# The first expert matrix in two transfers of 4 MB instead of four of 2 MB: a weight ring filled and freed by halves

## What is computed

```python
hdn = xb @ w_mlp1[e] + b_mlp1[e]          # w_mlp1[e]: 1024 x 2048, 8 MB
glu = jnp.minimum(hdn[:, :D_FF], SWIGLU_LIMIT)
lin = jnp.clip(hdn[:, D_FF:], -SWIGLU_LIMIT, SWIGLU_LIMIT)
act = glu * jax.nn.sigmoid(SWIGLU_ALPHA * glu) * (lin + 1.0)
return act @ w_mlp2[e] + b_mlp2[e]        # w_mlp2[e]: 1024 x 1024, 4 MB
```

## Time and profile before

| | us |
|---|---|
| median of 3 runs | 1193.2 (1192.66 to 1194.57) |
| the profiled execution | 1191.68 |
| its span, first to last instruction | 1189.9 |
| TensorE busy | 1093.7 (92%) |
| chain that ended last: DMA of the expert weights | 49% |
| chain: TensorE | 43% |
| mean granted TensorE clock | 0.993 |

### The profile page before, as it was taken

How to read it: one execution, slowest core, us unless ns; L and a number is a source line. 1 busy time by engine, 2 the same in 40 slices (tenths; PEclk the granted TensorE clock), 3 DMA queues, 4 the chain that set the end, 5 groups by cost and what they waited for, 6 DMA issues and landing times.

```text
span 1189.9 us, 14867 instructions
## 1 busy us (share of the span) xinstructions
PE 1093.7 (92%) x5421; PEld 493.3 (41%) x5422; DVE 367.6 (31%) x786; ACT 240.3 (20%) x332; POOL 3.6 (0%) x12
## 2 busy tenths in 40 slices
PE   9999998799999999999999999999888999999995
PEld 8888876543333333333333333333333333333332
DVE  6968773622211111111112212211111111111113
ACT  4846651301111111111111111111111111111112
POOL 1000000000000000000000000000000000000000
PEclk9999999899999999999999999999999999999998
DMA  9654447469999999999996999999999999999994
GB/s 339 197 173 150 164 146 261 195 281 428 428 430 426 431 427 428 430 427 430 429 426 256 431 425 431 428 427 432 426 429 431 425 431 427 427 432 425 430 429 188
DMA packets 45191, 439.44 MB, mean 369 GB/s; under 512 B 6044, under 2 KB 6232, under 8 KB 20504
## 3 DMA queue, kind: packets, MB, share of 16 engines
q1 hardware_dynamic: 43200, 436.16, 88.2%
q10 hardware_dynamic: 1976, 3.08, 0.8%
HBM read 438.17 MB, written 1.05 MB: 369 GB/s over the span
## 4 chain that ended last, share of the span: by engine, by line
DMA 51%; PE 43%; DVE 3%; ACT 2%; issue 1%; SPq 0%; DVEq 0%; ACTq 0%; PEldq 0%
DMA ring<-in_w_mlp_dram 49%; PE bank L964 19%; PE bank L648 8%; PE bank L989 6%; PE bank L642 2%; PE bank L817 2%; PE bank L882 2%; DMA sgm<-in_b_mlp_dram 1%; PE bank L922 1%; DMA ring<-in_w_in_dram 1%; PE bank L905 1%; ACT sgm L562 1%; ACT b1p L545 0%; PE bank L844 0%; PE bank L950 0%
## 5 line engine op out<-in xcount | busy, mean ns | idle before, releaser
L964 PE MATMUL bank<-ring,sga 128*64 128x512 f32 x2112 | 473.8, 595 | 62.2 <-DMA ring<-in_w_mlp_dram 62.2
L964 PEld LDWEIGHTS bank<-ring,sga 128*64 128x64 f32 x2112 | 146.9, 136 | 370.4 <-issue 238.0
L989 PE MATMUL bank<-ring,sgm 128*64 128x512 f32 x1056 | 233.9, 595 | 0.0
L1432 DVE TENSOR_SCALAR sga<-bank 128x512 f32<-128x512 f32 x33 | 22.8, 691 | 364.4 <-PE bank L964 364.4
L989 PEld LDWEIGHTS bank<-ring,sgm 128*64 128x64 f32 x1056 | 72.8, 137 | 136.1 <-issue 132.0
L569 ACT ACTIVATE sgm<-bank 128x512 f32<-128x512 f32 x33 | 19.7, 598 | 484.5 <-PE bank L964 484.5
L1452 DVE SCALAR_TENSOR_TENSOR moe_y_lo<-bank,slot_gate,moe_y_hi 128x512 fp32r<-128x512 f32 x33 | 24.8, 750 | 237.2 <-ACT moe_y_hi L576 237.2
L576 ACT ACTIVATE moe_y_hi<-bank,slot_gate 128x512 fp32r<-128x512 f32 x33 | 22.7, 687 | 259.3 <-PE bank L989 259.3
L882 PE MATMUL bank<-xn,hm 128*64 128x512 f32 x272 | 65.9, 605 | 1.3 <-DVE hm L1369 1.3
L1028 DVE TENSOR_TENSOR rlo<-ring,whi 128x2048 fp32r<-128x2048 f32 x26 | 58.9, 2285 | 5.6 <-ACT whi L416 5.3
L416 ACT ACTIVATE whi<-ring 128x2048 fp32r<-128x2048 f32 x26 | 49.0, 1917 | 7.4 <-PE bank L648 3.7
(11 more groups left out here) (260 smaller groups left out, 803.1 us busy)
## 6 DMA issues: line engine op xcount, KB each, us to landing
ring<-in_w_mlp_dram SPq DMA_DIRECT2D x192, 2048.0 KB, 23.5
ring<-in_w_in_dram SPq DMA_DIRECT2D x22, 1024.0 KB, 5.2
ring<-in_w_branch_dram SPq DMA_DIRECT2D x4, 1024.0 KB, 4.9
ring<-in_w_out_dram SPq DMA_DIRECT2D x4, 1024.0 KB, 4.9
xs<-in_x_dram SPq DMA_DIRECT2D x2, 512.0 KB, 3.8
out_dram<-xn ACTq DMA_DIRECT2D x2, 512.0 KB, 2.7
sgm<-in_b_mlp_dram ACTq DMA_DIRECT2D x3, 256.0 KB, 9.3
cst<-table_dram SPq DMA_DIRECT2D x1, 754.0 KB, 13.7
```

The lines of the kernel that those rows point to most:

```text
L964: last = mm(B[4 + u][g * C:(g + 1) * C, :], xgT[:, k % 4, k // 4, :], ring[:, q, u * FF + g * N:u * FF + (g + 1) * N], start=False, stop=( ...
L989: last = mm(B[7][g * C:(g + 1) * C, :], actT[:, j, h * C:(h + 1) * C], ring[:, q + j // 2, (j % 2) * D + g * N:(j % 2) * D + (g + 1) * N], ...
```

## The change

In `expert()` the first matrix goes in two transfers, each over two pairs (4 slots, one row of 32 KB per partition), and each waits until all four slots are freed; the second matrix goes as before. TensorE waits for landing at k = 0 and k = 4 alone, and counts four slots used at k = 3 and k = 7.

```diff
--- before.py
+++ after.py
@@ -73,6 +73,7 @@
 
 PAIRS = [SLOTS[Q_MOE + k] for k in range(0, PER_EXPERT, 2)]
 assert all(SLOTS[Q_MOE + 2 * i + 1] == at + 1 for i, at in enumerate(PAIRS))
+assert PAIRS[1] == PAIRS[0] + 2 and PAIRS[3] == PAIRS[2] + 2
 ROWS = 4
 
 
@@ -333,17 +334,16 @@
 
             def expert(e, freed):
 
-                for i, at in enumerate(PAIRS):
-                    sp.wait_ge(slots_used, freed(2 * i + 1))
-                    dst = ring[:, at:at + 2, :].rearrange("p a n -> p (a n)")
-                    if i < 4:
-                        g, half = i // 2, i % 2
-                        src = w_mlp1[0, e, g * N:(g + 1) * N, :].rearrange("(p s) n -> p (s n)", s=ROWS)
-                        src = src[:, half * 2 * SLOT:(half + 1) * 2 * SLOT]
-                    else:
-                        g = i - 4
-                        src = w_mlp2[0, e, g * N:(g + 1) * N, :].rearrange("(p s) n -> p (s n)", s=ROWS)
-                    sp.dma_start(dst, src).then_inc(landed[at], 16)
+                for g in range(2):
+                    at = PAIRS[2 * g]
+                    sp.wait_ge(slots_used, freed(4 * g + 3))
+                    src = w_mlp1[0, e, g * N:(g + 1) * N, :].rearrange("(p s) n -> p (s n)", s=ROWS)
+                    sp.dma_start(ring[:, at:at + HALF, :].rearrange("p a n -> p (a n)"), src).then_inc(landed[at], 16)
+                for g in range(2):
+                    at = PAIRS[4 + g]
+                    sp.wait_ge(slots_used, freed(KB + 2 * g + 1))
+                    src = w_mlp2[0, e, g * N:(g + 1) * N, :].rearrange("(p s) n -> p (s n)", s=ROWS)
+                    sp.dma_start(ring[:, at:at + 2, :].rearrange("p a n -> p (a n)"), src).then_inc(landed[at], 16)
 
             expert(0, lambda k: (Q_OUT, Q_OUT, Q_MOE)[k // 4])
             sp.wait_ge(tabled, 1)
@@ -957,15 +957,15 @@
                     if k == 1:
                         pe.wait_ge(yh_ready, i + 1)
                         pe.wait_ge(yl_ready, i + 1)
-                    if k % 2 == 0:
+                    if k % HALF == 0:
                         pe.wait_ge(landed[q], e * 16 + 16 * (loads_before(Q_MOE + k) + 1))
                     for u in range(2):
                         for g in range(2):
                             last = mm(B[4 + u][g * C:(g + 1) * C, :], xgT[:, k % 4, k // 4, :],
                                       ring[:, q, u * FF + g * N:u * FF + (g + 1) * N],
                                       start=False, stop=(k == KB - 1), skip_group_check=True)
-                    if k % 2:
-                        last.then_inc(slots_used, 2)
+                    if k % HALF == HALF - 1:
+                        last.then_inc(slots_used, HALF)
                 scatter(scat)
                 gather(2 * i + 4)
```

## The result

The change is slower: 1210.07 us in the median of 4 runs (1208.72 to 1210.80) against 1193.88 before (4 runs, 1192.66 to 1195.31), a ratio of 1.013 with a 95% interval of 1.0112 to 1.0147. The forecast was 1207.5, in a range of 1200 to 1213.

What follows compares the result with a forecast made beforehand. It took the saturated expert-weight DMA stream, with TensorE's work at its starts and ends, as the bound. 13.7 - 4.3 + 4.9 = +14.3 us on the profiled 1191.7 gave 1206.0, or 1207.5 against the median; range 1200 to 1213.

Steps and rivals of the forecast that it cites:

- First release: At item 0 and the second pass, the DMA idles 3.43 us longer until four slots are free: +6.9 us.
- Landing by halves: At expert 13's first pass and expert 31, 32 matmuls instead of 16 follow the last needed landing: +6.9 us.
- Longer rows: In the weight stream, 16 fewer packets per engine and expert and two fewer completions save 0.14 us per expert: -4.3 us.
- the ring: The expert-weight part from the first item on: 13.7 us lost by halves less 4.3 gained by longer rows.
- The bias load: In the front part, b_mlp1 lands later because it shares the engines with the first expert's longer rows: +4.9 us.
- each of the seven turns is 0.61 us longer: Per engine, seven weight rows alternate with bias rows; 32 KB rows lengthen the bias load's wait by 4.3 us.
- The rows already under way: Weight rows ahead of the first bias row took up to 2.7 us, and that may double.
- The bound itself: Upper limit on the bias delay: +7 us, as traffic beside it is over by 212.9 us.
- A: Rival at the front part: the bias load is not delayed, giving 1202.6 us; chance 0.20.
- B: Rival in the queue: 32 KB rows go as two packets, no gain or bias loss, 1206.6 us; chance 0.06.
- C: Rival on TensorE: its clock falls in longer waits, up to +14 us, half of it giving 1214.5; chance 0.08.
- D: Rival in the stream: a fixed cost per transfer, won back by fewer transfers, 1190.6 us at 0.35 each; chance 0.04.

Runs made afterwards that it cites:

- experiment 2: The kernel before with only SP changed, waiting until a whole half is freed, still 2 MB transfers: 1201.8 us, ratio 1.0061.
- experiment 1: The kernel before with only TensorE changed, waiting at k = 0 and k = 4 for both pairs of a half: 1202.45 us, ratio 1.0068.
- experiments 3: The kernel before with both SP and TensorE waiting for halves, still 2 MB transfers with 16 KB rows: 1208.91 us, ratio 1.0127.
- experiment 7: The change with each partition's 32 KB read as two 16 KB runs, so it does not compute the layer: 1210.31 us, ratio 1.0134.
- experiment 4: The change with the first expert's first matrix in four 2 MB transfers of 16 KB rows: 1205.45 us, ratio 1.0093.
- experiments 5 and 6: The kernel before, then the change, each issuing the first expert's weights only after the b_mlp1 copies landed: 1186.53 us and 1195.8 us.
- Experiment 8: The change with four spare matmuls on TensorE ahead of its wait at k = 4: 1208.99 us, ratio 1.0129.
- experiment 9: The kernel before with the bias landed first and first-matrix pairs 0 and 3 cut into single 1 MB slots: 1189.68 us, ratio 0.9959.

## Why the prediction was right

The four terms of the sum, one by one:

**First release, +6.9.** Right: experiment 2 gave +6.5. Together with the next term, the DMA's still time around the second pass grew from some 12 us (630.0 to 641.8) to 19 (640.4 to 659.1), by the 6.9 that were forecast.

**Landing by halves, +6.9.** Right: experiment 1 gave +7.2, both together +13.8 for the +13.7 of four times 3.43.

**Longer rows, -4.3.** Right in sign, size and cause: period 29.22 for 29.37, 4.6 us between experiments 3 and the change, and experiment 7 with the same transfers but 16 KB rows lost it again. Of the ring, 13.7 - 4.3 = 9.4 was forecast and 9.2 measured.

**The bias load, +4.9.** The mechanism was right (experiments 4 and 7), the size was short: +7.05 between the two profiles, and 7.1 by the medians of experiments 5 and 6. The mis-sized factor is "each of the seven turns is 0.61 us longer". Both queues together in the change, from 197.3 to 212.5 us:

```profile
q1 hardware_dynamic: 131, 3.77, 82.0%
q10 hardware_dynamic: 130, 0.79, 19.4%
```

131 packets of q1 are 115 rows (3.77 MB) and 16 completions, against 96 bias rows with their completions: the engines still take them one against one, and there are still some seven weight rows per engine. But a row took 82.0% x 16 x 15.2 / 115 = 1.73 us, where 16 KB took 0.93: 0.8 more, not 0.61. Bias rows were slower too: 19.4% x 16 x 15.2 / 96 = 0.49 us instead of 0.39 (27.3% x 16 x 8.6 / 96). Seven times 0.8 and six times 0.1 are 6.2 us of the 7.05.

The size differs between executions. Experiment 8 has the same transfers as the change and a piece of 17.21 us, 4.8 above that of before. From 197.3 to 210.6 us its queues have 128 packets each, 112 of them weight rows, again seven per engine, but a row takes 85.0% x 16 x 13.3 / 112 = 1.61 us: seven times 0.68 are 4.8. With 16 KB rows the pieces are 12.39 to 13.95 us in six profiles. The two kinds don't overlap, so the delay is sure, but one pair of profiles does not fix its size to better than about 2 us.

The rows already under way, of which I had counted up to 2.7 us more, did not grow at all: the first bias row came 3.5 us after its issue at 193.8, and 3.6 before. The 0.6 us that I had added to the turns for them made up for part of the longer turns, and that is luck. The bound itself was wrong as argued, too: it took the end of SP's traffic before (212.9) for fixed, while that traffic ended later here, at some 216 us.

The Trainium skill ("DMA: Bandwidth & Descriptors", section "Queues, rings and completion order") states that an engine typically drains some 9 to 17 descriptors of one ring before it switches. The price by that came nearer to the medians than mine, but its mechanism isn't seen: the trace does not agree. In every 1.9 us of the shared stretch both queues have rows, and near its end, from 208.7 to 210.6 us, they are still about even:

```profile
q1 hardware_dynamic: 14, 0.46, 78.3%
q10 hardware_dynamic: 12, 0.10, 17.5%
```

4.9 replaced by 7.05 and 9.4 by 9.2 is +16.2, the difference of the medians. The profiled execution shows 1.7 more because of a clock dip ahead of the bias: in nine of the twelve profiles the clock was at half once for 3.4 us in the mixer, somewhere between 40 and 170 us (twice in experiment 9), but never in the profiles of before and of experiments 6 and 7. The last of the three bias copies is issued at 193.1 to 193.6 us without the dip and at 194.8 to 195.2 with one.

**Rivals.** A (bias not delayed) and B (rows cut in two) are out by the 19.44 and by the packets. C is half true: the clock did fall, after waits of 2.6 us, in about every second item from 339 us on (0.98 in the stream). But a dip costs 1.6 us and not the 7 that I let it reach, and only if it falls on the first pass of expert 13 or on the last expert: never in the profile of the change, once in that of experiment 4, twice in that of 7, where it moved the execution by up to 3.3 us. With all of them removed, experiment 8, the ring is no faster. D (a fixed cost per transfer) is out by experiment 7, where transfers of 4 MB with 16 KB rows have the period of 2 MB, 29.36 us. The Trainium skill ("DMA: Bandwidth & Descriptors", section "Anatomy of one DMA — SWDGE (gpsimd) path") fits a fixed cost of 2.0 us per DMA for transfers that GpSimd issues. In SP's full queue no such cost is seen: with 8, 6 and 4 transfers per expert (experiment 9, before, and the change) the periods are 29.52, 29.37 and 29.22 us.

## What to carry to other kernels

Where a saturated stream runs through a ring of just one round, the size of the piece that is freed or awaited at once stands in the time, in matmuls, at each start and end of the stream, and no share of busy time shows it. In this kernel merging transfers gave back only some 9 ns per row saved (4.6 us in all), and splitting them further uncovered the next release. Before long rows go into a queue, see who else uses the DMA engines then. A short load on the chain that is taken in turns with them waits for their length. Here issuing it first was worth 7.2 us before and 14.3 in the change, more than any gain in the ring.

## What the runs showed of the hardware

- A 16 KB row takes 614 ns on a DMA engine in the stream; the periods of 29.22, 29.37 and 29.52 us go with 32, 48 and 64 rows per engine and expert, 0.15 us for 16 rows with 2 completions.
- SP's and ScalarE's queues were served packet by packet in turn: 112 rows of 16 KB to 96 of 8 KB, 115 rows of 32 KB to 96 of 8 KB, and with the completions 128 packets to 128, 131 to 130, and 96 to 96. Beside the other queue a weight row took 30 to 50% longer than alone (0.93 for 0.61 us; 1.61 to 1.73 for 1.22).
- The same bias load beside the same rows took 12.39 to 13.95 us (16 KB rows, six profiles) and 17.21 or 19.44 us (32 KB rows).
- 0.90 MB, most of it in three copies into 32 partitions each, went at some 225 GB/s with no other traffic.
- TensorE idle for 2.6 us in every 29.2 was followed by a fall of the granted clock to its lower level for 3.4 us in about every second item; with waits of 1.24 us, or with 1.9 us of spare matmuls in the same wait, it never fell in the stream.
